# Hybrid layer with a 32-expert MoE on one core: the expert rows turned by VectorE in squares of 32 in place of TensorE transposes

## The chip, the core and the metric

One core of a Trainium2 chip runs the whole layer in one launch. The metric is the device time of that launch in microseconds. The engines that matter here are TensorE (PE, with its weight loads shown apart as PEld), VectorE (DVE), ScalarE (ACT) and the SyncE queue (SP), which issues nearly all of the DMAs.

## The reference, cut to what matters

The layer is a gated hybrid block (gMLP and windowed attention) for 256 positions of width 1024, followed by a mixture of experts: each of the 256 rows goes to its 4 best of 32 experts. All weights are f32. What the change touches is the expert part:

```python
xb = h_pad[slot_tok].reshape(n_blocks, MOE_BLOCK, d)      # rows gathered by expert
def expert_block(args):
    xblk, e = args
    gu = xblk @ w_gate_up[e] + b_gate_up[e]               # 1024 -> 2048
    g = jnp.minimum(gu[:, :D_FF], SWIGLU_LIMIT)
    u = jnp.clip(gu[:, D_FF:], -SWIGLU_LIMIT, SWIGLU_LIMIT)
    hid = g * jax.nn.sigmoid(SWIGLU_ALPHA * g) * (u + 1.0)
    return hid @ w_down[e] + b_down[e]                    # 1024 -> 1024
```

The results are added back to the rows with their gate weights, and a final RMSNorm follows.

## The kernel before

**Stages.** The first 320 us compute the conditioning, the gated block, the router and its tables. Then come the experts, about 1293 us into the span, and a short tail (RMSNorm, store).

**Blocks.** The kernel gathers rows in blocks of 32 (`BM`). With these inputs there are 50 blocks for 32 experts, taken expert by expert; an expert has one to five blocks. Since a block has only 32 rows, each product is cut into four column quarters (`NG` = 4) which run side by side on TensorE in tiles of 128x32: quarter q of the output columns lies in PSUM partitions 32q to 32q+31. So one block's gate-up result is 128 partitions x 512 (256 gate columns, 256 up columns) and its hidden rows `hid` are 128x256. Quarter q holds columns 256q to 256q+255.

**One block on PE** (function `expert`): 8 gate-up steps over the 128-row chunks of the contraction (line 1700), each of 4 matmuls of 512 columns (in f32 each is two MATMUL instructions, 64 in all); the bias (1707); `combine` of the previous block into the accumulator (1663); `gather` of the next block's rows by a one-hot matrix (1645); two transposes of the combine map `selg` (1720); two transposes of `hid` (1725); `gather_T`, two transposes of the gathered rows `xe` (1651); 8 down steps (1735, 64 instructions).

**The other engines in a block.** DVE turns the gate-up result into `hid` (1270 to 1277), copies the gathered rows to `xe` (1280), copies the combine map (1284) and scales the down result (1286). ACT computes the sigmoid (748), then copies the transposed `hid` from PSUM to `hidT` (751) and the transposed rows to `xT` (755). `hidT` and `xT` are the stationary operands of the down and gate-up products.

**Weights.** Each expert has 12 pieces of 1 MB (8 of gate-up, 4 of down), all 384 loaded by SP in order into 22 slots (`SLOTS`) of SBUF. Lines 373 and 379 issue a gate-up or a down piece. A slot is refilled when its piece has been used in the *last* block of its expert: SP waits on `gu_used` or `down_used` for that count (`refill`, `used`). Until an expert's last block, its 12 slots are held.

**The start of the experts.** DVE builds the tables: the block map (1177 and around), the slots of each row (1185 to 1187, twice), the expert of each block (1194, 1196, event `table_ready`), and the order of the experts (`last_is_least`, 1203 to 1241, event `order_ready`), on which SP's refills wait. DVE works its instructions in the order written. At the same time PE gathers block 0 (1645), ACT copies it (740), PE turns it (1651) and ACT copies it to `xT` (742).

Of the kernel before, what the change touches and what calls it, by code (L numbers as in the profile page):

```python
# [15 lines left out]
P = 128  # L16
D = 1024
# [20 lines left out]
HW = D // NG  # L38
KG = HW // P
QR = 32  # L40
# [11 lines left out]
          "down_used", "ex_ready", "exp_done", "g_ready", "gates_ready", "gt_done", "gT_ready",  # L52
          "gu_used", "h2_ready", "heads_ready", "hid_ready", "hidT_ready", "hot_ready", "ht_done", "hT_parts",
          "mask_ready", "merged_ready", "mod_col_ready", "modT_done", "mT_parts", "negm_ready", "negtop_ready",
# [3 lines left out]
          "u_ready", "v_gelu", "var_ready", "vec_steps", "vn_ready", "vp_ready", "w_lower_dve", "w_lower_pool",  # L58
          "w_upper_ready", "ws_masked", "x2_ready", "xe_ready", "xg_done", "xn_ready", "xt_done", "xT_ready",
          "y_out", "y_ready", "yaT_parts", "ybT_parts")  # L60


def bass_hybrid_layer(nc, x, c, positions, w_ada, b_ada, g_norm1, w_in, b_in, ln_v_g, ln_v_b,
# [46 lines left out]
    with ctx:  # L110
# [68 lines left out]
        rope_room = spare[:, 1024:1536]  # L179
        xT = mod[:, 8:10, :].rearrange("p i (q n) -> p i q n", q=NG)  # L180
        y_sb = mod[:, 0:2, :].rearrange("p a b -> p (a b)")
        hidT = mod[:, 6:8, :].rearrange("p i (q n) -> p i q n", q=NG)
        gt2 = mod[:, 10:12, :].rearrange("p a b -> p (a b)")
# [27 lines left out]
        onehot = cut(BM // 2).bitcast(BF16)  # L211
        xe = cut(HW)
        gT = cut(TILES * P)
# [351 lines left out]
        def _(act):  # L565
# [167 lines left out]
            for t in range(TILES):  # L733
# [4 lines left out]

            act.wait_ge(ev("xg_done"), 1)
            act.activation(xe, banks[6][:, 0:HW], ACT.Copy).then_inc(ev("xe_ready"), 1)  # L740
            act.wait_ge(ev("xt_done"), 1)
            act.activation(xT.rearrange("p i q n -> p (i q n)"), banks[6][:, 0:KG * P], ACT.Copy)\
               .then_inc(ev("xT_ready"), 1)
            act.wait_ge(ev("table_ready"), 1)
            total = act.value_load(table[0:1, TOTAL_AT:TOTAL_AT + 1], min_val=1, max_val=GMAX - 1)
            with act.Fori(0, total) as g:
                act.wait_ge(ev("g_ready"), g + 1)
                act.activation(g_sig, g_cap, ACT.Sigmoid, scale=ALPHA).then_inc(ev("sig_ready"), 1)  # L748

                act.wait_ge(ev("ht_done"), g + 1)  # L750
                act.activation(hidT.rearrange("p i q n -> p (i q n)"), banks[7][:, 0:KG * P], ACT.Copy)\
                   .then_inc(ev("hidT_ready"), 1)

                act.wait_ge(ev("xt_done"), g + 2)
                act.activation(xT.rearrange("p i q n -> p (i q n)"), banks[6][:, 0:KG * P], ACT.Copy)\
                   .then_inc(ev("xT_ready"), 1)

# [9 lines left out]
        def _(dve):  # L767
# [381 lines left out]
            def gather_map(g, slots):  # L1149
# [99 lines left out]
            with dve.Fori(0, total) as g:  # L1249
# [50 lines left out]
        def _(pe):  # L1300
# [340 lines left out]
            def gather():  # L1641

                for t in range(TILES):
                    for q in range(NG):
                        last = pe.matmul(banks[6][q * BM:(q + 1) * BM, 0:HW], sel[:, t, :], h2[:, t, q * HW:(q + 1) * HW],  # L1645
                                         start=(t == 0), stop=(t == 1), skip_group_check=True)
# [25 lines left out]
            z_put(last, "etab")  # L1672
            pe.wait_ge(ev("xe_ready"), 1)
            gather_T()
            pe.wait_ge(ev("bias_part_ready"), 4)
# [4 lines left out]
            def expert(e, s, turns):  # L1680


                def piece(i):
                    at = PIECES * s + i
                    pe.wait_ge(slot_in[at % SLOTS], turns * 16 + (16 * (at // SLOTS) + 16))
                    return store(at % SLOTS).rearrange("p (a n) -> p a n", a=2)

# [4 lines left out]
                with pe.Fori(0, blocks) as b:  # L1692
# [4 lines left out]
                    for k in range(KC):  # L1697
                        w = piece(k)
                        for q in range(NG):
                            last = pe.matmul(banks[4][q * BM:(q + 1) * BM, :], xT[:, k % KG, k // KG, :],  # L1700
                                             w[:, :, q * HW:(q + 1) * HW],
                                             start=(k == 0), stop=(k == KC - 1), skip_group_check=True)
                        last.then_inc(ev("gu_used"), 1)
                        if k == 0:
                            for a in range(2):
                                for q in range(NG):
                                    pe.matmul(banks[4][q * BM:(q + 1) * BM, a * HW:(a + 1) * HW], onehot,
                                              bias_parts[a][:, q * HW:(q + 1) * HW], start=False, stop=False,
                                              skip_group_check=True)
# [12 lines left out]

                    pe.wait_ge(ev("hid_ready"), g + 1)
# [4 lines left out]
                    gather_T()  # L1728

                    pe.wait_ge(ev("hidT_ready"), g + 1)  # L1730
                    for i in range(KC // 2):
                        w = piece(KC + i)
                        for k in (2 * i, 2 * i + 1):
                            for q in range(NG):
                                last = pe.matmul(banks[7][q * BM:(q + 1) * BM, 0:HW], hidT[:, k % KG, k // KG, :],  # L1735
                                                 in_groups(w[:, k % 2, :])[:, q],
                                                 start=(k == 0), stop=(k == KC - 1), skip_group_check=True)
# [38 lines left out]
```

## Time and profile before

| | us |
|---|---|
| median of 3 runs (lowest to highest) | 1309.48 (1308.46 to 1310.32) |
| the profiled execution's own time | 1308.77 |
| its span, first to last instruction | 1307.0 |
| PE busy | 1067.9 (82%) |
| DVE busy | 440.1 (34%) |
| ACT busy | 202.4 (15%) |
| bytes read from HBM | 470.98 MB, 361 GB/s over the span |

What lies outside of the span is 1.8 us. The 40 slices of the profile's page are 32.7 us each. The shares of busy time are averages over stages with different limits: PE is busy four fifths of the time, but in the expert stage the DMA engines are at 416 to 418 GB/s in most slices. Releasers of waits are inferred, and matmul ends are modelled.

### The profile page before, as it was taken

How to read it: one execution, taken by the hardware profiler on the slowest of the kernel's cores; microseconds unless marked ns; L12 is line 12 of the kernel's file. 1: busy time of each engine (PE TensorE's matmuls, PEld its weight loads, DVE VectorE, ACT ScalarE, POOL GpSimd, SP SyncE). 2: the span in 40 equal slices, each digit the busy share in tenths (PEclk: the TensorE clock that was granted, in tenths of full speed). 3: DMA queues.
4: the chain of work that ended last, by engine and by line, in shares of the span. 5: the costliest groups of instructions: out<-in, count | busy, mean ns of one | idle time of the engine just before them, and what ended most of it. 6: DMA issues, size and time to landing. Idle time of an engine off the chain costs nothing.

```text
span 1307.0 us, 26543 instructions
## 1 busy us (share of the span) xinstructions
PE 1067.9 (82%) x10210; PEld 495.3 (38%) x10211; DVE 440.1 (34%) x1057; ACT 202.4 (15%) x376; POOL 93.2 (7%) x41
## 2 busy tenths in 40 slices
PE   3689999996999768675799999899776679966784
PEld 1457677883343213111244434343211124421231
DVE  1588588876332112111132322223211113211122
ACT  2112033133111101000021112021100001200011
POOL 0154344300000000000000000000000000000000
PEclk9799999996999769877999999999878879987887
DMA  8897865778999999999979999929999997999996
GB/s 305 254 336 260 312 229 213 218 291 324 384 415 416 416 418 417 417 418 416 416 292 417 417 416 418 417 99 399 416 417 417 418 417 301 417 418 416 417 417 262
DMA packets 113523, 473.22 MB, mean 362 GB/s; under 512 B 12832, under 2 KB 16800, under 8 KB 80544
## 3 DMA queue, kind: packets, MB, share of 16 engines
q1 hardware_dynamic: 110880, 469.03, 89.9%
q10 hardware_dynamic: 2560, 3.02, 0.9%
q8 instruction: 60, 0.98, 0.3%
q14 instruction: 23, 0.19, 0.0%
HBM read 470.98 MB, written 1.05 MB: 361 GB/s over the span
## 4 chain that ended last, share of the span: by engine, by line
PE 34%; SPq 30%; DMA 27%; issue 4%; DVE 3%; ACT 2%; POOL 1%; ACTq 0%; DVEq 0%
SPq L379 13%; SPq L373 12%; PE acc L1338 11%; DMA gate_up<-in_w_down_dram 10%; PE bank L1700 10%; DMA gate_up<-in_w_gate_up_dram 6%; PE bank L1735 5%; DMA down<-in_w_gate_up_dram 3%; DMA down<-in_w_down_dram 2%; DMA gate_up<-in_w_ada_dram 2%; DMA x_sb<-in_w_gate_up_dram 1%; PE acc L1663 1%; DMA room<-in_w_gate_up_dram 1%; PE bank L1645 1%; SPq L368 1%
## 5 line engine op out<-in xcount | busy, mean ns | idle before, releaser
L1700 PE MATMUL bank<-gate_up,mod 128*32 128x512 f32 x2512 | 345.7, 673 | 103.0 <-DMA gate_up<-in_w_gate_up_dram 84.3
L1700 PEld LDWEIGHTS bank<-gate_up,mod 128*32 128x32 f32 x2512 | 75.9, 115 | 313.5 <-DMA gate_up<-in_w_gate_up_dram 178.3
L1735 PE MATMUL bank<-gate_up,mod 128*32 128x256 f32 x2528 | 152.5, 385 | 29.4 <-DMA gate_up<-in_w_down_dram 25.9
L1338 PE MATMUL acc<-gate_up_r 128*128 128x512 f32 (+1 forms) x544 | 136.9, 397 | 15.7 <-DVE gate_up_r L777 12.2
L748 ACT ACTIVATE front<-front 128x256 f32<-128x256 f32 x50 | 20.8, 417 | 743.6 <-DVE front L1270 743.6
L1270 DVE TENSOR_SCALAR front<-bank 128x256 f32<-128x256 f32 x50 | 21.2, 425 | 325.1 <-PE bank L1700 325.1
L1338 PEld LDWEIGHTS acc<-gate_up_r 128*128 128x128 f32 x544 | 100.1, 192 | 44.1 <-issue 21.6
L1735 PEld LDWEIGHTS bank<-gate_up,mod 128*32 128x32 f32 x2528 | 75.5, 110 | 94.9 <-DMA gate_up<-in_w_down_dram 39.0
L1286 DVE TENSOR_TENSOR mod<-bank,mod 128x256 f32<-128x256 f32 x50 | 21.2, 425 | 244.4 <-PE bank L1735 244.4
L348 POOL TENSOR_TENSOR gate_up_r<-gate_up,gate_up_r 128x2048 fp32r<-128x2048 f32 (+1 forms) x14 | 88.7, 6339 | 116.6 <-DVE gate_up_r L777 116.6
L1700 PE MATMUL bank<-down,mod 128*32 128x512 f32 x448 | 62.6, 671 | 18.6 <-DMA down<-in_w_gate_up_dram 16.1
L1190 DVE TENSOR_SCALAR front<-front 128x2 f32 x100 | 22.9, 229 | 154.0 <-issue 152.5
L1338 PE MATMUL acc<-gate_up_r,down_r 128*128 128x512 f32 (+1 forms) x272 | 66.7, 388 | 0.0
L1663 PE MATMUL acc<-mod,front 32*128 32x256 f32 x816 | 65.3, 439 | 0.5 <-DVE mod L1286 0.5
L748 ACT ACT_TABLE_LOAD x50 | 64.2, 1283 | 1.7 <-issue 0.8
L1663 PEld LDWEIGHTS acc<-mod,front 32*128 32x128 f32 x816 | 40.8, 205 | 52.7 <-issue 49.5
L1645 PE MATMUL bank<-h,front 128*32 128x256 f32 x816 | 56.0, 393 | 0.5 <-DVE front L1151 0.5
L1338 PEld LDWEIGHTS acc<-gate_up_r,down_r 128*128 128x128 f32 x272 | 51.2, 192 | 10.7
L777 DVE CAST gate_up_r<-gate_up 128x4096 fp32r<-128x4096 f32 (+1 forms) x17 | 42.3, 2488 | 16.0 <-DMA gate_up<-in_w_in_dram 15.2
L348 DVE TENSOR_TENSOR gate_up_r<-gate_up,gate_up_r 128x2048 fp32r<-128x2048 f32 (+2 forms) x17 | 44.3, 2606 | 0.6
L1735 PE MATMUL bank<-down,mod 128*32 128x256 f32 x512 | 31.5, 382 | 11.5 <-DMA down<-in_w_down_dram 11.1
L1700 PEld LDWEIGHTS bank<-down,mod 128*32 128x32 f32 x448 | 13.2, 114 | 57.1 <-DMA down<-in_w_gate_up_dram 33.0
(303 smaller groups left out, 817.1 us busy)
## 6 DMA issues: line engine op xcount, KB each, us to landing
gate_up<-in_w_gate_up_dram SPq DMA_DIRECT2D x186, 1024.0 KB, 20.5
gate_up<-in_w_down_dram SPq DMA_DIRECT2D x96, 1024.0 KB, 23.8
down<-in_w_gate_up_dram SPq DMA_DIRECT2D x46, 1024.0 KB, 20.6
gate_up<-in_w_ada_dram SPq DMA_DIRECT2D x12, 2048.0 KB, 9.0
down<-in_w_down_dram SPq DMA_DIRECT2D x22, 1024.0 KB, 25.6
gate_up<-in_w_in_dram SPq DMA_DIRECT2D x10, 2048.0 KB, 14.2
x_sb<-in_w_gate_up_dram SPq DMA_DIRECT2D x12, 1024.0 KB, 21.7
room<-in_w_gate_up_dram SPq DMA_DIRECT2D x12, 1024.0 KB, 22.1
```

The source lines that it names most:

```text
L348: return eng.tensor_tensor(w_lower[i % RING][:, chunks, 0:cols], ring[i % RING][:, chunks, 0:cols], w_upper[i % 2][:, chunks, 0:cols], ALU ...
L373: eng.dma_start(store(at % SLOTS), w_gu_view[:, bass.ds(e, 1), k, :].rearrange("p a n -> p (a n)"))\
L379: eng.dma_start(store(at % SLOTS).rearrange("p (a n) -> p a n", a=2), w_dn_view[:, bass.ds(e, 1), 2 * i:2 * i + 2, :].rearrange("p a k n - ...
L748: act.activation(g_sig, g_cap, ACT.Sigmoid, scale=ALPHA).then_inc(ev("sig_ready"), 1)
L777: return dve.tensor_copy(dst, src)
L1190: return dve.tensor_scalar(slots, slots_gates[:, bass.ds(e, 1), 0:2].rearrange("p a t -> p (a t)"), slot_base[:, bass.ds(g, 1)], None, ALU ...
L1270: dve.tensor_scalar(g_cap, banks[4][:, 0:HW], LIMIT, None, ALU.min).then_inc(ev("g_ready"), 1)
L1338: last = pe.matmul(bank[:, 0:cols], lhsT[:, k, rows], w[:, k, 0:cols], start=(n == 0 and k == 0), stop=(n == 2 and k == KC - 1))
L1645: last = pe.matmul(banks[6][q * BM:(q + 1) * BM, 0:HW], sel[:, t, :], h2[:, t, q * HW:(q + 1) * HW], start=(t == 0), stop=(t == 1), skip_g ...
L1663: last = pe.matmul(acc[:, q, t * HW:(t + 1) * HW], gT[rows, t * P:(t + 1) * P], y_sb[rows, :], start=False, stop=True, skip_group_check=True)
L1700: last = pe.matmul(banks[4][q * BM:(q + 1) * BM, :], xT[:, k % KG, k // KG, :], w[:, :, q * HW:(q + 1) * HW], start=(k == 0), stop=(k == K ...
L1735: last = pe.matmul(banks[7][q * BM:(q + 1) * BM, 0:HW], hidT[:, k % KG, k // KG, :], in_groups(w[:, k % 2, :])[:, q], start=(k == 0), stop ...
```

## The change

The four transposes of f32 squares of 128x128 in each block are dropped from TensorE. VectorE turns `hid` into `hidT` and the gathered rows into `xT` with its own transpose, which turns each square of 32x32 in place of its own. For the squares to land where the products need them, the columns of the quarters are dealt out differently: quarter q now holds the columns 128c + 32q + n (c counting the 128-column chunks, n from 0 to 31), so it takes runs of 32 columns, one from each chunk, where it took one run of 256. This is `in_squares`. Gate-up, its bias and the gather read their moving operands that way; the down product keeps its columns. ACT's two copies go, `xe` goes, and so do the events `ht_done`, `xt_done` and `xe_ready`.

```diff
+        def in_squares(rows):
+            return rows.rearrange("p (c q n) -> p q c n", q=NG, n=BM)
...
-                act.wait_ge(ev("ht_done"), g + 1)
-                act.activation(hidT.rearrange("p i q n -> p (i q n)"), banks[7][:, 0:KG * P], ACT.Copy)\
-                   .then_inc(ev("hidT_ready"), 1)
-
-                act.wait_ge(ev("xt_done"), g + 2)
-                act.activation(xT.rearrange("p i q n -> p (i q n)"), banks[6][:, 0:KG * P], ACT.Copy)\
-                   .then_inc(ev("xT_ready"), 1)
...
+            def rows_T():
+                return dve.transpose(xT.rearrange("p c n -> p (c n)"), banks[6][:, 0:HW])
...
             bias_map(0).then_inc(ev("hot_ready"), 1)
+            dve.wait_ge(ev("xg_done"), 1)
+            rows_T().then_inc(ev("xT_ready"), 1)
...
                 dve.tensor_tensor(hid, hid, g_sig, ALU.mult).then_inc(ev("hid_ready"), 1)
+                dve.wait_ge(ev("hid_ready"), g + 1)
+                dve.transpose(hidT.rearrange("p c n -> p (c n)"), hid).then_inc(ev("hidT_ready"), 1)
                 dve.wait_ge(ev("xg_done"), g + 2)
-                dve.tensor_copy(xe, banks[6][:, 0:HW]).then_inc(ev("xe_ready"), 1)
+                rows_T().then_inc(ev("xT_ready"), 1)
...
-            def gather_T():
-                for i in range(KG):
-                    last = pe.transpose(banks[6][:, i * P:(i + 1) * P], xe[:, i * P:(i + 1) * P], ident[:, :])
-                last.then_inc(ev("xt_done"), 1)
...
-                            last = pe.matmul(banks[4][q * BM:(q + 1) * BM, :], xT[:, k % KG, k // KG, :],
-                                             w[:, :, q * HW:(q + 1) * HW],
+                            last = pe.matmul(banks[4][q * BM:(q + 1) * BM, :], xT[:, k, :],
+                                             in_squares(w)[:, q],
...
-                    for i in range(KG):
-                        last = pe.transpose(banks[7][:, i * P:(i + 1) * P], hid[:, i * P:(i + 1) * P], ident[:, :])
-                    last.then_inc(ev("ht_done"), 1)
-                    pe.wait_ge(ev("xe_ready"), g + 2)
-                    gather_T()
                     pe.wait_ge(ev("hidT_ready"), g + 1)
```

PE within one block, from the end of gate-up to the down product, before:

```order
L1700 MATMUL bank<-gate_up,mod 32x512 x28
L1663 MATMUL acc<-mod,front 128x256 x8
L1715 REGISTER_ALU
L1645 MATMUL bank<-h,front 32x256 x8
L1720 MATMUL bank<-ident,front 128x128 x2
L1725 MATMUL bank<-ident,front 128x128 x2
L1651 MATMUL bank<-ident,front 128x128 x2
L1735 MATMUL bank<-gate_up,mod 32x256 x32
```

and the same place in the change (its line numbers are its own):

```order
L1692 MATMUL bank<-gate_up,mod 32x512 x28
L1657 MATMUL acc<-mod,front 128x256 x8
L1707 REGISTER_ALU
L1644 MATMUL bank<-h,front 32x256 x8
L1712 MATMUL bank<-ident,front 128x128 x2
L1720 MATMUL bank<-gate_up,mod 32x256 x32
```

The two pairs of transposes between the one of `selg` and the down product are gone. DVE in one block, from the gate-up result to the down result, before:

```order
L1270 TENSOR_SCALAR front<-bank 128x256
L1271 TENSOR_SCALAR front<-bank 128x256
L1177 ISA
L1177 TENSOR_SCALAR front<-front 96x32
L1274 SCALAR_TENSOR_TENSOR front<-front 128x256
L1277 TENSOR_TENSOR front<-front 128x256
L1279 REGISTER_ALU
L1280 COPY front<-bank 128x256
L1284 COPY front<-bank 128x256
```

and in the change:

```order
L1266 TENSOR_SCALAR front<-bank 128x256
L1267 TENSOR_SCALAR front<-bank 128x256
L1170 ISA
L1170 TENSOR_SCALAR front<-front 96x32
L1270 SCALAR_TENSOR_TENSOR front<-front 128x256
L1273 TENSOR_TENSOR front<-front 128x256
L1276 STREAM_TRANSPOSE mod<-front 128x256
L1278 REGISTER_ALU
L1167 STREAM_TRANSPOSE mod<-bank 128x256
L1283 COPY front<-bank 128x256
```

One transpose has come in behind the making of `hid`, and the copy to `xe` has become a transpose to `xT`. At the start of the experts DVE has in the change:

```order
L1173 SCALAR_TENSOR_TENSOR front<-front 128x64
L1174 MEMSET front 32x16
L1170 TENSOR_SCALAR front<-front 96x32
L1167 STREAM_TRANSPOSE mod<-bank 128x256
```

The last of these four is new; it stands between the block map and the slots of each row, and waits for the gather of block 0.

## Rows read from the trace of the kernel before

**Rows 1.** The page, part 2: GB/s moved in each fortieth of the span.

```profile
GB/s 305 254 336 260 312 229 213 218 291 324 384 415 416 416 418 417 417 418 416 416 292 417 417 416 418 417 99 399 416 417 417 418 417 301 417 418 416 417 417 262
```

**Rows 2.** Windows: length; PE, PEld, DVE, ACT, POOL busy; PEclk, DMA share, GB/s.

```profile
865.00:880.00 15.00, 14.93 (x200) 6.69 (x196) 4.25 (x14) 2.60 (x5) 0.00 (x0) 1.00 0.00 0
```

**Rows 3.** Chain that ended last, at three stretches: start us, us, what.

```profile
644.36 1.07 PE bank L1735 x16
...
655.65 3.66 PE bank L1735 x64
...
669.54 3.66 PE bank L1735 x64
...
674.27 6.01 PE bank L1700 x56
...
836.47 1.07 PE bank L1735 x16
...
849.61 3.66 PE bank L1735 x64
...
863.49 3.66 PE bank L1735 x64
...
877.37 3.66 PE bank L1735 x64
...
882.11 6.01 PE bank L1700 x56
...
1072.96 1.07 PE bank L1735 x16
...
1084.25 3.66 PE bank L1735 x64
...
1098.13 3.66 PE bank L1735 x64
...
1102.87 6.01 PE bank L1700 x56
```

**Rows 4.** Waits of the SP queue: who for whom, us in total, times, longest.

```profile
SPq L379 <- PE bank L1700: 123.9, 11, 47.0
```

**Rows 5.** Timeline of one block: start, us, engine line op, count, idle before.

```profile
812.61 1.07 PE L1645 MATMUL bank<-h,front 128*32 128x256 f32 x16
812.93 0.43 DVE L1277 TENSOR_TENSOR front<-front 128x256 f32<-128x256 f32 x1
...
813.75 0.42 DVE L1280 COPY front<-bank 128x256 f32<-128x256 f32 x1 [0.39 <-PE bank L1645]
...
813.89 0.38 PE L1725 MATMUL bank<-ident,front 128*128 128x128 f32 x2
...
814.23 0.44 PE L1651 MATMUL bank<-ident,front 128*128 128x128 f32 x2
814.30 0.38 ACT L751 ACTIVATE mod<-bank 128x256 f32<-128x256 f32 x1 [1.76 <-PE bank L1725]
...
814.74 0.83 PE L1735 MATMUL bank<-gate_up,mod 128*32 128x256 f32 x9
```

**Rows 6.** Timeline at the start of the experts, all engines.

```profile
321.88 0.18 DVE L1185 SCALAR_TENSOR_TENSOR front<-front 128x32 f32<-128x32 f32 x1
...
322.27 0.38 ACT L740 ACTIVATE front<-bank 128x256 f32<-128x256 f32 x1 [3.77 <-PE bank L1645]
...
325.90 1.93 PE L1700 MATMUL bank<-gate_up,mod 128*32 128x512 f32 x8 [2.45 <-issue]
...
328.81 0.21 DVE L1241 TENSOR_TENSOR table<-front 1x64 int32<-1x64 f32 x1
...
331.43 1.08 SPq L379 DMA_DIRECT2D gate_up<-in_w_down_dram  x2
```

**Rows 7.** Windows at the same place, columns as in rows 2.

```profile
330.00:332.00 2.00, 2.00 (x24) 0.49 (x16) 0.40 (x1) 0.00 (x0) 0.00 (x0) 1.00 0.12 49
```

**Rows 8.** Timeline near the end: four VectorE operations of 512 columns each.

```profile
1301.21 2.73 DVE L1294 SCALAR_TENSOR_TENSOR h<-acc,sm,gate_up 128x512 f32<-128x512 f32 x4
```

More of the change, by code:

```diff
@@ L38 @@
 HW = D // NG
-KG = HW // P
 QR = 32
@@ L52 @@
           "down_used", "ex_ready", "exp_done", "g_ready", "gates_ready", "gt_done", "gT_ready",
-          "gu_used", "h2_ready", "heads_ready", "hid_ready", "hidT_ready", "hot_ready", "ht_done", "hT_parts",
+          "gu_used", "h2_ready", "heads_ready", "hid_ready", "hidT_ready", "hot_ready", "hT_parts",
           "mask_ready", "merged_ready", "mod_col_ready", "modT_done", "mT_parts", "negm_ready", "negtop_ready",
@@ L58 @@
           "u_ready", "v_gelu", "var_ready", "vec_steps", "vn_ready", "vp_ready", "w_lower_dve", "w_lower_pool",
-          "w_upper_ready", "ws_masked", "x2_ready", "xe_ready", "xg_done", "xn_ready", "xt_done", "xT_ready",
+          "w_upper_ready", "ws_masked", "x2_ready", "xg_done", "xn_ready", "xT_ready",
           "y_out", "y_ready", "yaT_parts", "ybT_parts")
@@ L179, in bass_hybrid_layer @@
         rope_room = spare[:, 1024:1536]
-        xT = mod[:, 8:10, :].rearrange("p i (q n) -> p i q n", q=NG)
+        xT = mod[:, 8:10, :].rearrange("p i (c n) -> p (i c) n", n=BM)
         y_sb = mod[:, 0:2, :].rearrange("p a b -> p (a b)")
-        hidT = mod[:, 6:8, :].rearrange("p i (q n) -> p i q n", q=NG)
+        hidT = mod[:, 6:8, :].rearrange("p i (c n) -> p (i c) n", n=BM)
         gt2 = mod[:, 10:12, :].rearrange("p a b -> p (a b)")
@@ L211, in bass_hybrid_layer @@
         onehot = cut(BM // 2).bitcast(BF16)
-        xe = cut(HW)
         gT = cut(TILES * P)
@@ L736, in _ @@
             act.activation(gT, bank[:, 0:TILES * P], ACT.Copy).then_inc(ev("gT_ready"), 1)
-            act.wait_ge(ev("xg_done"), 1)
-            act.activation(xe, banks[6][:, 0:HW], ACT.Copy).then_inc(ev("xe_ready"), 1)
-            act.wait_ge(ev("xt_done"), 1)
-            act.activation(xT.rearrange("p i q n -> p (i q n)"), banks[6][:, 0:KG * P], ACT.Copy)\
-               .then_inc(ev("xT_ready"), 1)
             act.wait_ge(ev("table_ready"), 1)
@@ L1644, in gather @@
                     for q in range(NG):
-                        last = pe.matmul(banks[6][q * BM:(q + 1) * BM, 0:HW], sel[:, t, :], h2[:, t, q * HW:(q + 1) * HW],
+                        last = pe.matmul(banks[6][q * BM:(q + 1) * BM, 0:HW], sel[:, t, :], in_squares(h2[:, t, :])[:, q],
                                          start=(t == 0), stop=(t == 1), skip_group_check=True)
                 last.then_inc(ev("xg_done"), 1)
-            def gather_T():
-                for i in range(KG):
-                    last = pe.transpose(banks[6][:, i * P:(i + 1) * P], xe[:, i * P:(i + 1) * P], ident[:, :])
-                last.then_inc(ev("xt_done"), 1)
             def combine():
@@ L1672, in _ @@
             z_put(last, "etab")
-            pe.wait_ge(ev("xe_ready"), 1)
-            gather_T()
             pe.wait_ge(ev("bias_part_ready"), 4)
@@ L1685, in piece @@
                     pe.wait_ge(slot_in[at % SLOTS], turns * 16 + (16 * (at // SLOTS) + 16))
-                    return store(at % SLOTS).rearrange("p (a n) -> p a n", a=2)
+                    return store(at % SLOTS)
                 if s:
@@ L1707, in expert @@
                                     pe.matmul(banks[4][q * BM:(q + 1) * BM, a * HW:(a + 1) * HW], onehot,
-                                              bias_parts[a][:, q * HW:(q + 1) * HW], start=False, stop=False,
+                                              in_squares(bias_parts[a])[:, q], start=False, stop=False,
                                               skip_group_check=True)
@@ L1734, in expert @@
                             for q in range(NG):
-                                last = pe.matmul(banks[7][q * BM:(q + 1) * BM, 0:HW], hidT[:, k % KG, k // KG, :],
-                                                 in_groups(w[:, k % 2, :])[:, q],
+                                last = pe.matmul(banks[7][q * BM:(q + 1) * BM, 0:HW], hidT[:, k, :],
+                                                 in_groups(w[:, k % 2 * D:(k % 2 + 1) * D])[:, q],
                                                  start=(k == 0), stop=(k == KC - 1), skip_group_check=True)
```

4 lines of the change are left out of this document (removed).

## The prediction

> **What bounds the kernel now.** I read the bytes per slice first [rows 1]. From slice 11 on, where the experts are under way, the core moves 415 to 418 GB/s in nearly every slice and never more. TensorE is busy most of that time, but each expert's 12 MB take about 30 us at that rate, and a block of PE work takes 13.9 us (669.54 less 655.65) [rows 3], so an expert of one or two blocks is waited for by PE, not by the DMA. The DMA is the bound of the stage. Four slices fall out of line: 292, 99, 399 and 301 GB/s. Against 417 they lack 0.30, 0.76, 0.04 and 0.28 of 32.7 us, some 45 us in which no weights move. In the middle of the longest gap the window shows DMA share 0.00 with PE at 14.93 of 15.00 us [rows 2]. SP's waits say why: its refills wait for PE's gate-up steps, up to 47 us at a time [rows 4]. These are the experts with four or five blocks: all 22 slots are full, and none comes free before the expert's last block. Only there does PE's speed count.
>
> **How many blocks count.** The chain of waits [rows 3] shows the three stretches. Each begins with a down piece of 16 instructions that PE had to wait for (644.36, 836.47, 1072.96), so what PE saved earlier is lost in that wait. It ends when the last block's gate-up steps release slots (about 674, 881 and 1102 us). Whole down products between these points: 2, 3 and 2, the seven rows of 3.66 us. Whatever lets the down product start earlier counts 7 times, not 50 times. In the other 43 blocks it turns into a longer wait for weights, or into slots released to a DMA that is busy anyway.
>
> **Part 1, the transposes in a block: -0.76 us each.** In the block shown [rows 5], `hid` is ready at 812.93 + 0.43 = 813.36. The down product starts at 814.74: between them stand PE's turn of `hid` (813.89), which had queued behind other PE work, PE's turn of the rows (814.23), which waited for DVE's copy to end at 814.17, and ACT's copy, which ended at 814.68. In the change two things must end. On DVE, a transpose of 128x256 starts at about 813.40. No row shows this operation. The nearest rows are 128x256 operations from SBUF and from PSUM, 0.43 and 0.42 us [rows 5]; I take 0.43, which gives 813.83, and with the 0.06 us that PE took to follow DVE here (814.17 to 814.23), 813.89. On PE, the `selg` transposes are past at 813.89, where the first turn of `hid` started. Then the tile shape changes to 128x32, which costs about 0.1: the 16 gather instructions take 1.00 to the next shape (812.61 to 813.61), where by the down rows 16 take 4 x 0.216 = 0.86 (64 in 3.66, 16 in 1.07, so 48 in 2.59). That gives 813.98, and PE's side is the later one. So 814.74 - 813.98 = 0.76. The turn of the rows goes behind that of `hid` on DVE and is done near 814.3; `xT` is wanted only after the down product. DVE's copy of the combine map moves from 814.15 to about 814.3, also in time. ACT has only the sigmoid left, on the path as before. Seven times 0.76 is **-5.3 us**.
>
> The value of that transpose, T, is the term to bound. DVE's side is 813.46 + T, so the saving is 1.28 - T, and at most 0.76. From below T can't help beyond that. From above, if 4-byte data goes through twice, T grows by 256 elements: 512 columns take 2.73 / 4 = 0.68 [rows 8], so T = 0.43 + 0.26 = 0.69 and the saving is 0.59. If four times, T = 1.2 and the saving is 0.08.
>
> The Trainium skill, page "VectorE: DVE Perf Modes", section "The three transpose paths", gives 311 ns for 128 columns of bf16 on VectorE and 390 ns on TensorE, a gain of 0.08 us and no figure for f32. By that difference alone seven blocks would give only 0.6 us; the trace shows that what goes is two copies and two hand-overs more than a transpose.
>
> **Part 2, the moving operands in runs of 32: 0.** Gate-up and gather now read 16 and 8 runs of 128 bytes. Rows of before have runs of 256 and 128 columns alone: the gather reads one run of 256 per instruction, the down product two of 128, and 16 instructions take 1.07 us in both [rows 3, 5]. So the number of runs costs nothing between one and two, and I carry that on to 16. It can't be a gain. As a loss it has no bound from these rows, and it is the first rival.
>
> The Trainium skill, page "Advanced Engine Details and Errata", section "Memory Cachelines", says that SBUF reads run at full rate as long as at least two accesses fall into one 16-byte line. Runs of 128 bytes satisfy that, so by the page the cost is 0; no run here shows it yet.
>
> **Part 3, the start: +0.85 us.** The new wait stands in DVE's chain of tables. DVE reached line 1185 at 321.88; now it waits until the gather of block 0 is done, 322.27 (where ACT's copy started) [rows 6], turns the rows for 0.43 and goes on at 322.73, 0.85 later. Queued behind it is the whole chain to `order_ready` (328.81), for which SP waits, and the table on which PE's first block waits (325.90). SP's first refill is at 331.43, and the DMA idles before it: share 0.12 [rows 7]. Nothing hides this; the DMA streams without a break from there to the first stretch, so the whole shift reaches the end. PE's turn and ACT's copy, which go, were beside this chain. With T = 0.69 the term is 1.1. At least it is about 0.4 (a turn in no time), if the wait stands.
>
> **Part 4, nothing.** The tail (last down piece, norm, store) is untouched. The granted clock in the stretches is 1.00 [rows 2] with PE at work nearly without a break, and four short instructions fewer in 13.9 us leave it so.
>
> **Sum.** -5.32 + 0.85 = -4.5 us. Against the profiled execution's 1308.77 that is 1304.3. That execution lies 0.7 below the median of 1309.48, so for a median I give 1305.0. A measurement of this kernel can tell about 0.2% (2.6 us) from no change.
>
> **Rivals.**
>
> *Short runs slow the moving reads (ends slower).* In the three stretches lie 7 whole gate-up products of 16 groups of four instructions, and 2 groups in each last block, 118 groups of 0.43 us (56 instructions, 14 groups, in 6.01) [rows 3]. The gain of 4.5 us is used up at 38 ns a group, 9%, or 2.7 ns for each of 14 further runs. Four streams now read within the same 512 bytes of a partition, where they were 1 KB apart. At 5 ns a run it is +8.3, 1313; at half rate (+50 us) about 1355. For it: no row has runs under 128 columns. Against it: one and two runs cost the same. 0.10.
>
> *The transpose of f32 takes two passes.* Part 1 gives 7 x 0.59 = 4.1, part 3 1.1: 1306.5. 0.13.
>
> *It takes four passes.* -0.6 + 1.6, so +1.0: 1310.5. From T = 1.08 on the change doesn't pay. 0.04.
>
> *The saving doesn't reach the DMA.* If SP's own steps (table loads before each refill) set the resumption and not PE, or if the DMA gap closes later by what it opens later, only part 3 or little more is left: 1308 to 1310. Against it: SP waits for PE in so many words, up to 47 us [rows 4]. 0.13.
>
> *The forecast:* 1305.0, its own range 1303.5 to 1306.3. 0.60.
>
> **Range and chances.** I leave out the short runs at a real price and the four passes, and little below the forecast: 1303.0 to 1310.0. Faster by over 0.2% means under 1306.9: 0.57 of the forecast and 0.08 of the two passes, 0.65. Slower by over 0.2% (over 1312.1): most of the short runs and a little for what I don't see, 0.13. The rest, 0.22, is within.
>
> **What would show it.** In the block of the changed profile: the down product starts about 0.6 us after `hid`'s last multiplication, the block period within an expert is 13.1 in place of 13.9, STREAM_TRANSPOSE takes 0.4 to 0.5 us, and 56 gate-up instructions still take 6.01 us. At the start: `order_ready`'s write and the first refill 0.8 to 0.9 later. In the page: the same slices below 417 GB/s, their gap shorter by 5 us in sum. A longer gate-up product, or a transpose near 1 us, would prove me wrong; so would an unchanged gap.

## The result, and the profile after

| | before | after |
|---|---|---|
| median, this comparison (lowest to highest) | 1309.07 (1308.46 to 1310.32) | 1300.16 (1299.88 to 1302.20) |
| profiled execution | 1308.77 | 1300.29 |
| its span | 1307.0 | 1298.5 |

The ratio is 0.9936, 95% interval 0.9921 to 0.9951, from four runs of each: 8.9 us less, where the forecast had 4.5 and the range ended at 1303.0. A second set of runs of the same kernel gave 1301.69, so part of the 8.9 us is chance; how much is taken up below.

The page of the changed kernel, part 2, GB/s in each fortieth, to be laid beside [rows 1]:

```profile
GB/s 309 244 337 272 301 227 222 207 290 334 361 416 417 416 416 416 417 417 418 416 311 417 416 417 417 416 169 416 417 417 417 417 418 317 415 417 418 417 417 257
```

The same slices fall out of line: 292 has become 311, 99 and 399 have become 169 and 416, 301 has become 317. At 417 GB/s for a slice of 32.7 us that is 1.5, 6.8 and 1.3 us less of gap: the two outer ones about as forecast (2 x 0.76 = 1.5 each), the middle one three times the forecast (3 x 0.76 = 2.3).

One block of the changed kernel, timeline, beside [rows 5]:

```profile
809.50 1.07 PE L1644 MATMUL bank<-h,front 128*32 128x256 f32 x16
809.82 0.43 DVE L1273 TENSOR_TENSOR front<-front 128x256 f32<-128x256 f32 x1
810.28 0.45 DVE L1276 STREAM_TRANSPOSE mod<-front 128x256 f32<-128x256 f32 x1
...
810.51 0.44 PE L1712 MATMUL bank<-ident,front 128*128 128x128 f32 x2
810.65 0.44 DVE L1167 STREAM_TRANSPOSE mod<-bank 128x256 f32<-128x256 f32 x1
...
810.87 1.50 PE L1720 MATMUL bank<-gate_up,mod 128*32 128x256 f32 x24
811.05 0.42 DVE L1283 COPY front<-bank 128x256 f32<-128x256 f32 x1
```

`hid` is ready at 809.82 + 0.43 = 810.25, its turn takes 0.45, and the down product starts at 810.87, 0.62 after `hid`; before it was 814.74 - 813.36 = 1.38. The chain of waits of the changed kernel at the three stretches, beside [rows 3]:

```profile
645.52 1.07 PE bank L1720 x16
...
656.12 3.59 PE bank L1720 x64
...
669.24 3.59 PE bank L1720 x64
...
833.24 1.07 PE bank L1720 x16
...
843.84 3.59 PE bank L1720 x64
...
856.96 3.59 PE bank L1720 x64
...
870.08 3.59 PE bank L1720 x64
...
1065.75 1.07 PE bank L1720 x16
...
1076.35 3.59 PE bank L1720 x64
...
1089.48 3.59 PE bank L1720 x64
```

A block takes 669.24 - 656.12 = 13.12 (13.88 before), the same seven down products count, and the gate-up products between them take as long as before: the chain has 56 of their instructions at 6.01 us in every block. The start of the experts, beside [rows 6]; the first line is the gather of block 0 in before, the others are of the changed kernel:

```profile
320.27 1.94 PE L1645 MATMUL bank<-h,front 128*32 128x256 f32 x16 [0.54 <-DVE front L1151]
...
320.68 1.94 PE L1644 MATMUL bank<-h,front 128*32 128x256 f32 x16 [0.88 <-DVE front L1140]
...
322.67 0.45 DVE L1167 STREAM_TRANSPOSE mod<-bank 128x256 f32<-128x256 f32 x1 [0.31 <-PE bank L1644]
...
329.94 0.21 DVE L1237 TENSOR_TENSOR table<-front 1x64 int32<-1x64 f32 x1
...
332.57 1.08 SPq L381 DMA_DIRECT2D gate_up<-in_w_down_dram  x2
```

`order_ready` is written 1.13 later and the first refill goes out 1.14 later than before (forecast 0.85). Of this 0.41 lies ahead of the wait: the gather of block 0 began at 320.68 in this execution, before at 320.27. The wait and the turn cost the other 0.72 or so.

**Where the time went.** The trace records when each of the 16 DMA engines lands its part of each 1 MB piece. I worked out, for every piece, the landing of the first and the last engine, and then the shift of the first against the kernel before. Between the stretches, where the DMA streams without a break, this shift stays within about 0.2 us; it changes only at the start and in the three stretches:

```
                 start   stretch 1  stretch 2  stretch 3
after - before   +1.2      -1.4       -7.0       -1.2
forecast         +0.85     -1.5       -2.3       -1.5
```

The four add up to 8.4 of the 8.5 us by which the span is shorter. All of the excess over the forecast, 4.7 us, is in the second stretch. Two things fill it. (I call restart the moment at which TensorE goes on after its wait for the last down piece of a long expert, in that expert's first block.) First, the piece that ends the wait at the second restart (piece 215, the last of the twelve of the five-block expert) lands 4.51 us after its first engine's part in before, and 1.63 us after it in the change. The chain shows the restart at 833.24 in place of 836.47, though the first engine is ahead by only 0.36: 2.9 us. Second, TensorE's granted clock. Before, the chain at the restart reads:

```profile
811.92 24.50 DMA down<-in_w_down_dram
...
836.47 1.07 PE bank L1735 x16
837.54 1.69 PE bank L1700 x8
...
839.66 6.81 PE bank L1700 x56
```

and the windows of the kernel before at the same place (columns as in [rows 2]; the seventh number is the granted clock):

```profile
834.00:838.00 4.00, 1.53 (x20) 0.68 (x24) 0.39 (x1) 0.00 (x0) 0.00 (x0) 0.97 1.01 419
838.00:842.00 4.00, 4.00 (x33) 1.60 (x29) 0.90 (x6) 0.00 (x0) 0.00 (x0) 0.61 1.01 420
```

TensorE had stood idle for the piece (1.53 of 4.00 us busy), at 837.7 the granted clock fell from 2.4 to 1.2 GHz for 3.4 us, and 8 gate-up instructions took 1.69 where they take 0.86. From the restart to the first whole down product it was 849.61 - 836.47 = 13.14 us; in the first stretch, at full clock, 655.65 - 644.36 = 11.29 [rows 3]: 1.85 us lost. In the changed kernel the windows are at 1.00:

```profile
834.00:838.00 4.00, 4.00 (x52) 1.50 (x48) 0.55 (x2) 0.00 (x0) 0.00 (x0) 1.00 1.01 416
838.00:842.00 4.00, 4.00 (x44) 1.44 (x40) 1.76 (x8) 0.08 (x1) 0.00 (x0) 1.00 1.00 416
```

3 x 0.76 + 2.88 + 1.85 = 7.0, as found. That is an account of two executions. Whether the two extra terms belong to the change is what the later experiments ask.

### The profile page after: what moved, and what is told of

Its sections match the earlier page's. It is cut to its first block, busy times and chain, and to the rows that moved or that the text cites. A ratio compares the mean times of both kernels' runs of the same rounds, so it can differ in the third digit from the quotient of the medians.

```text
span 1298.5 us, 26038 instructions
## 1 busy us (share of the span) xinstructions
PE 1049.3 (81%) x10008; PEld 474.0 (37%) x10009; DVE 458.5 (35%) x1108; ACT 163.4 (13%) x274; POOL 93.2 (7%) x41
## 4 chain that ended last, share of the span: by engine, by line
PE 39%; DMA 29%; SPq 24%; issue 3%; DVE 3%; ACT 1%; POOL 1%; ACTq 0%; DVEq 0%
PE bank L1692 13%; PE acc L1337 11%; DMA gate_up<-in_w_down_dram 11%; SPq L381 11%; SPq L375 9%; DMA gate_up<-in_w_gate_up_dram 9%; PE bank L1720 6%; DMA down<-in_w_down_dram 4%; DMA room<-in_w_gate_up_dram 2%; PE acc L1657 2%; PE bank L1644 2%; DMA gate_up<-in_w_ada_dram 2%; DMA down<-in_w_gate_up_dram 1%; DMA gate_up<-in_w_in_dram 1%; PE bank L1359 1%
## 5 line engine op out<-in xcount | busy, mean ns | idle before, releaser
L1692 PE MATMUL bank<-gate_up,mod 128*32 128x512 f32 x2512 | 352.4, 683 | 100.3 <-DMA gate_up<-in_w_gate_up_dram 81.5
L1720 PE MATMUL bank<-down,mod 128*32 128x256 f32 x512 | 33.2, 394 | 13.5 <-DMA down<-in_w_down_dram 13.5
```

The costliest lines, as they stand in the source:

```text
L1692: last = pe.matmul(banks[4][q * BM:(q + 1) * BM, :], xT[:, k, :], in_squares(w)[:, q], start=(k == 0), stop=(k == KC - 1), skip_group_chec ...
```

## The experiments

Four theories are named in the expectations. A and B are about one block, L and U about how many blocks count. A: the saving is the step from `hid` to the down product, so both turns must go. B: each turn saves its own part. L: seven blocks count, and the rest of the gain is the late piece and the clock. U: some twelve blocks count, and the gain is paid by the shorter block alone.

### One part of the change alone

Only the rows: `hid` is turned by TensorE and copied by ACT as before.

```diff
-                dve.tensor_copy(xe, banks[6][:, 0:HW]).then_inc(ev("xe_ready"), 1)
+                rows_T().then_inc(ev("xT_ready"), 1)
...
-                    pe.wait_ge(ev("xe_ready"), g + 2)
-                    gather_T()
```

> The gathered rows are turned by VectorE (also block 0's), hid still goes TensorE, PSUM, ScalarE. Theory A (the saving per block is the step from hid to the down product, and both old turns must go for it): the down product still waits for ScalarE's copy of hidT, so the block period inside an expert stays 13.88 us, and only the start costs +1.1: about 1310.0. Theory B (each turn taken from TensorE saves its own part): period 13.5 and about 1306.5.

Measured: 1308.35 median of 10 runs, ratio 0.9991 (0.9978 to 1.0004), between A's 1310.0 and B's 1306.5. The chain of this kernel in the first stretch:

```profile
656.42 0.39 ACT mod L750
...
656.86 3.66 PE bank L1728 x64
...
670.74 3.66 PE bank L1728 x64
```

The block is 13.88, as before: ACT's copy of `hid` still ends the wait for the down product, so the rows' turn alone saves nothing.

Only `hid`: the rows go by DVE's copy, TensorE and ACT as before; gate-up and its bias read in runs of 32.

```diff
-                    for i in range(KG):
-                        last = pe.transpose(banks[7][:, i * P:(i + 1) * P], hid[:, i * P:(i + 1) * P], ident[:, :])
-                    last.then_inc(ev("ht_done"), 1)
...
+                dve.transpose(hidT.rearrange("p c n -> p (c n)"), hid).then_inc(ev("hidT_ready"), 1)
```

> hid is turned by VectorE, the gathered rows still go VectorE copy, TensorE, ScalarE. Theory A: TensorE's turn of the rows now waits behind VectorE's turn of hid and its copy (about 814.3 in the block shown) and the down product starts at about 814.7 as before: period 13.85, no cost at the start, about 1308.5. Theory B: period 13.4 and about 1305.0.

Measured: 1307.11 (10 runs), ratio 0.9980 (0.9967 to 0.9993). The chain in the first stretch:

```profile
654.67 0.42 DVE front L1283
...
655.13 0.44 PE bank L1654 x2
655.57 3.59 PE bank L1734 x64
...
669.31 3.59 PE bank L1734 x64
```

13.74, a saving of 0.14. DVE copies the rows only after it has turned `hid` (654.30 + 0.45), so TensorE's turn of the rows now waits for DVE and stands in the path in place of `hid`. In the block A holds: 0.00 and 0.14 alone, 0.76 together. Both times lie 1.4 to 1.7 us under those that A gave; the account of all profiles below has where the rows' one gains in its profile, at a restart and not in a block. The 56 gate-up instructions are 6.01 in both kernels.

### The start

The change, with block 0's rows copied by ACT and turned by TensorE, so that DVE doesn't wait.

```diff
-            dve.wait_ge(ev("xg_done"), 1)
-            rows_T().then_inc(ev("xT_ready"), 1)
...
+            pe.wait_ge(ev("xe_ready"), 1)
+            gather_T()
```

> The change, but block 0's rows are copied by ScalarE and turned by TensorE as before, so VectorE's table chain at the start has no wait. Theory A: the 1.15 us at the start reach the end: about 1299.0, with the period at 13.12. Rival: the start is absorbed by a later wait for weights, and the time stays at 1300.2.

> The kernel with the old start once more, unchanged: in its first profile the weights landed 2.1 us earlier than in the change up to the second restart, and 1.2 later after it. Theory L: the first holds again (it is the start's wait), the second doesn't (it was half clock on the restart), so over ten runs it lies at or below the change by about 1 us. Rival: the loss at the restart is there again and the old start brings nothing.

Measured: 1301.85 (4 runs, ratio 0.9940, 0.9919 to 0.9962) and 1302.07 (5 runs, 0.9955, 0.9941 to 0.9969), where the expectations had 1299.0 and about 1 us under the change: both missed. In the profiles the block is 13.12 and the weights run 0.9 ahead of before in the one and 0.8 behind it in the other; in the four other profiles of kernels without the wait (before_again, hid_only and the two padded kernels before, below) they run 0 to 1.3 behind. So the start scatters between executions by as much as the cost in question. The seven profiles with the wait stand 0.9 behind before on average, the seven without it (before itself among them) 0.3, which is in favour of a cost of 0.6 but lies within that scatter. The mean of these nine runs is 1302.0 (within about 1.0 either way, 95%) and that of the 17 runs that have the wait (the change twice, and twice with padding, below) 1301.95 (within about 0.8). The wait's 0.7 us is plain in the trace of after; the times show no sign of it, but they couldn't tell 0.7 from nothing.

### Adding to the block

The change, with two (or four) chained copies of `hid` ahead of its turn on DVE, which do nothing but delay the turn.

```diff
+                dve.tensor_copy(xe, hid).then_inc(ev("dose"), 1)
+                dve.wait_ge(ev("dose"), g * 2 + 1)
+                dve.tensor_copy(xe, hid).then_inc(ev("dose"), 1)
+                dve.wait_ge(ev("dose"), g * 2 + 2)
```

> The change with two added VectorE copies of hid (0.47 us each, one after the other) in front of hid's turn, in each block: the down product starts about 0.8 later, so the period is again 13.9, while the rest of the change stands. Theory L (7 blocks of 0.76 count; the other 4.4 us of the gain come from where a late weight piece and a stretch of half clock happened to fall in the kernel before): 1306 to 1310, by whether a piece lands late at the second restart. Theory U (more than 7 blocks carry the saving to the end, about 12): the period alone decides, and the time is before's plus the start's 1.15, 1310.2, with no late piece.

> As dose2 with four added copies: the down product starts 0.94 later than in dose2, the period is 14.6. Theory L (7 blocks count): 1308.0 + 6.6 = 1314.6. Theory U (12 blocks count): 1308.0 + 11.3 = 1319.3.

Measured: two copies 1308.01 (ratio 0.9993, 0.9984 to 1.0003), block 13.70, within L's range and under U's 1310.2; four copies 1309.96 (1.0007, 0.9994 to 1.0020), block 14.35, under both (L 1314.6, U 1319.3), ten runs each. With four copies the chain of a block is DVE's:

```profile
653.80 0.44 DVE front L1274
...
654.26 0.31 DVE front L1277
...
655.25 0.30 DVE front L1283
655.58 0.46 DVE mod L1285
...
656.08 3.66 PE bank L1729 x64
```

From two to four copies a block grows by 0.65 and the time by 2.0, where seven blocks make 4.5. From the change to two copies a block grows by 0.58 and the time by about 6, where seven blocks make 4.1. Neither theory gives both. The two profiled executions are the fastest of its ten (1306.12) and the slowest of its ten (1312.39); what their traces have is in the account below. The medians are left unexplained: they don't follow the block's length in a straight line.

### The same two kernels again

No edit; the change and the kernel before, with nothing different.

> The change itself once more, unchanged, for a second profile and more times. Theory L: its block period is 13.12 again, and what remains of the gain over the counted 4.2 us differs from profile to profile, since it comes from how late the last of 16 DMA engines delivers at the second restart and whether half clock falls on it: single times spread over 1299 to 1303, the median near 1300.5. Theory U: every profile shows the same 8.5 us, and the times stay within 1 us of each other.

> The kernel before once more, unchanged, for a second profile. Theory L: period 13.88; the 3.3 us lost at the second restart (a piece landing 1.5 late, 1.84 of half clock) need not be there again in that form. Theory U: the second restart looks the same.

Measured: 1301.69 (5 runs, ratio 0.9951, 0.9938 to 0.9965) and 1308.19 (10 runs, 0.9996). The profile of the kernel before repeats itself: spread of piece 215 at 4.30, clock at 1.2 GHz from 837.9 for 3.4 us, a second stretch within 0.2. The profile of the change doesn't. Its first and third stretch gain 1.45 and 1.7 again, but the second 4.7 in place of 7.0, and the windows say why:

```profile
830.00:834.00 4.00, 3.42 (x32) 1.19 (x28) 0.26 (x1) 0.00 (x0) 0.00 (x0) 0.50 1.04 423
834.00:838.00 4.00, 4.00 (x40) 1.32 (x36) 0.84 (x5) 0.00 (x0) 0.00 (x0) 0.76 1.01 418
```

The spread is 1.83, near the 1.63 of the first profile, so the piece came early; but the clock fell at 829.1 for 6.8 us, over the restart. In its chain the first 16 down instructions take 1.94 where they took 1.07. So the full clock at the restart isn't part of the change. The span is the same to 0.2 us all the same (1298.7), since the start of this execution is 1.7 earlier: that both profiles show the same total is luck. The times lie from 1300.40 to 1303.96, not within 1 us of each other as U had it; L had 1299 to 1303 and a median near 1300.5.

### Moving the loads of instructions

In the profile's queues stand 60 loads of instructions of 16 KB in before:

```profile
q8 instruction: 60, 0.98, 0.3%
```

By the trace's records the median of them takes 1.08 us (0.88 to 1.47). The spread of the pieces grows in steps of 0.7 to 1.8 us, nearly all of them within 5 us behind such a load (694.3 behind 691.7, 836.4 behind 833.3; the step at 682.8, right behind a stretch, has none), and falls to 0.1 to 0.5 in each stretch in which the DMA stands still. Most loads make no such step: between 700 and 830 us seven loads come in before, and the spread stays at 3.0. But what the 16 parts of a piece lag behind its first, added up, grows by 1 to 2 us behind each of them (from 13.5 to 15.0 us behind the one at 810.8). That is what would be seen if a load delays one engine at a time and the piece comes later only when it is the one that is last already; the records don't name the engine. In before a load at 833.3 is followed by a step from 3.04 to 4.51 at piece 215 itself. In the change, one at 834.3 comes after the piece has landed. The rest of the difference at piece 215 is older: the spread ahead of it was 3.0 in before and 1.6 in the change since 695 us.

The Trainium skill, page "Runtime: NRT & Kernel Launch", section "Instruction fetch mechanics", says that instructions are refilled in blocks of 16 KiB over a DMA queue and that crossing a block's border is mostly hidden. The size agrees with the trace (60 loads, 0.98 MB); what the traces here add is a delay of weight pieces.

To move the loads, tiny products near the start of TensorE's program, where it waits for its first rows anyway (32 of them, or 96), are added to the kernel before and to the change.

```diff
             pe.wait_ge(ev("consts"), 3)
+            for _ in range(32):
+                pe.matmul(banks[6][0:BM, 0:BM], ident[:, 0:BM], ident[:, 0:BM], start=True, stop=True)
             pe.wait_ge(ev("xn_ready"), TILES)
```

> The kernel before with 32 tiny products of ident by ident (32x32) added to TensorE's program near its start, in time in which TensorE waits for the first rows; nothing else changes, and their result is used by nobody. They only shift where TensorE's later instructions lie, and so when the 16 KB loads of instructions come. In the profiles of the kernel before such a load at 833.3 us falls into the wait for the last down piece ahead of the second stretch (piece 215, whose slowest DMA engine lands 4.51 us behind the fastest), in the change one at 834.3 falls behind it (1.63 us). Theory L (7 blocks times 0.76 us, and the rest of the gain is this piece and the half clock behind it): if the load moves out of 830 to 836 us, the spread of piece 215 is 1.6 to 3.1, the second stretch starts 1.4 to 2.9 us earlier, and the time is 1305.5 to 1308; if it doesn't move, all stays as before, 1308 to 1310. Theory U (the extra gain is paid by the shorter blocks themselves): 1308.5 to 1309.5 either way, the second stretch where it was.

> The same with 96 tiny products (about three times the shift). Theory L: as for 32, a spread of piece 215 of 1.6 to 3.1 and 1305.5 to 1308 where the load of instructions leaves 830 to 836 us, 1308 to 1310 where it does not. Theory U: 1308.5 to 1309.5 either way. Should the 96 products not fit into the wait (some 11 us), all is later by up to 2 us.

> The change with 32 tiny products of ident by ident in the same place. Theory L: part of the second stretch's gain hangs on where the load of instructions falls; with it at 834.3 or later the time stays at 1300 to 1302; with it in 829 to 833 us piece 215 lands with a spread of 3.1 or more and the time is 1301.5 to 1304.5. The gain in the first and third stretch (1.5 us each) and the block of 13.12 us don't move. Theory U: 1300 to 1301.5 wherever the load falls.

> The change with 96 tiny products. As for 32: by L 1300 to 1302 with the load of instructions at 834.3 or later, 1301.5 to 1304.5 with it in 829 to 833 us; by U 1300 to 1301.5 wherever it falls. Up to 2 us more if the 96 products don't fit into the wait.

Measured: before with 32, 1308.09 (ratio 0.9996, 0.9981 to 1.0011); with 96, 1308.38 (0.9995, 0.9983 to 1.0006), ten runs each; the change with 32, 1303.51 (0.9953, 0.9935 to 0.9971); with 96, 1302.42 (0.9946, 0.9928 to 0.9964), four runs each. None of the four medians is in U's ranges (1308.5 to 1309.5 for before, 1300 to 1301.5 for the change); the two of the change are in L's 1301.5 to 1304.5. In the profiles of both padded kernels before no load lies between 828 and 895 us, and the spread of piece 215 is 1.72 and 1.95. The chain of the one with 32:

```profile
811.05 22.98 DMA down<-in_w_down_dram
834.03 0.04 issue
834.08 1.70 PE bank L1737 x16
835.78 1.71 PE bank L1702 x8
...
837.91 6.01 PE bank L1702 x56
```

The restart is 2.4 us earlier than in before, at the same length of block, with the first engine 0.4 later: how late the piece is hangs on where the loads of instructions fall, as L said, and a few instructions 800 us earlier move them. In the change with 32 the load lies at 829.5, ahead of the piece, and the spread steps up to 2.98; with 96 it lies at 832.1, also ahead of it, and the spread stays at 1.95, where L had 3.1 or more. So a load ahead of the piece makes it late only sometimes, as above. But L's 1305.5 to 1308 for the padded kernels before is met by neither median. The profiles, one execution each, show what took the gain there: the clock fell at 1069.9 for 3.4 us, which makes the third stretch 1.3 us longer, and with 96 at 645.3 and, for 6.8 us, at 1071.9 (the stretches 1.5 and 3.0 us longer). With 32 it was low at the very end too. The last down piece and the last `combine`, first in before and then with 32:

```profile
1293.72 1.11 PE bank L1735 x16
...
1295.34 1.19 PE acc L1663 x16
...
1292.82 1.98 PE bank L1737 x16
...
1295.30 2.14 PE acc L1665 x16
```

That is 1.8 us behind the last stretch, and it isn't of the change.

The account of all the profiles, by the same working as above:

```
us against before   start  str. 1  str. 2  str. 3     end  spread 215  clock at 1.2 GHz at a restart
before_again         0.8    0.0    -0.2    -0.1      +0.2    4.30      837.9 (3.4)
before_pad32         0.2   +0.3    -2.9    +1.3      +2.0    1.72      834.4 (3.4), 1069.9 (3.4)
before_pad96         1.3   +1.5    -2.7    +3.0      -0.2    1.95      645.3, 836.4 (3.4), 1071.9 (6.8)
rows_only            1.2    0.0    -2.6    +1.3      -0.1    3.65      1070.7 (3.4)
hid_only             0.0   -0.3    -0.8    -0.2      -0.3    3.21      833.6 (6.8)
dose2                1.6   -0.3    -3.4    -0.5       0.0    1.93      834.6 (3.4)
dose4                0.0   +0.8    -1.3    +1.5      +2.6    1.68      none
after                1.2   -1.4    -7.0    -1.2      -0.1    1.63      none
after_again         -0.5   -1.5    -4.7    -1.7       0.0    1.83      829.1 (6.8)
after_pad32          1.5   -1.5    -3.7    -1.5       0.0    2.98      831.8 (6.8)
after_pad96          1.4   +0.9    -6.7    -1.6       0.0    1.95      643.8 (6.8)
start_old           -0.9   -1.5    -3.5    -1.4      -0.2    3.36      832.8 (3.4)
start_again          0.8   -1.5    -6.8    -1.5      +2.2    1.87      none
```

`end` is what is left of the difference of the spans. Where it is over 2, in before_pad32, dose4 and start_again, the last piece landed later behind its first part than in before (by 0.2 to 1.1 us) and the clock was at 1.2 GHz on the last products, which took 1.3 to 1.8 us longer.

Each cell of a stretch is the sum of three things: the blocks, the spread of the piece and the clock at the restart. For the second stretch I took 3 times the difference of the block, the difference of the spread, and for the clock what the time from the restart to the next down product has over that of an undisturbed restart of the same kernel. That gives each of the cells within 0.2 (in the kernel before with 96, where no restart is undisturbed, with that of before), but for dose4: -1.3 where the sum is -3.3. There TensorE didn't wait for the piece, which had landed at 834.4; the down product that it belongs to began only at 833.86:

```profile
833.86 3.66 PE bank L1729 x64
```

and reached the piece at 836.5. With blocks this long work ahead of the restart is no longer lost in the wait, so the seven are right only as long as TensorE waits there.

Every kernel with the whole change has -1.2 to -1.7 in the first and the third stretch, two blocks of 0.76, with one exception, and there the clock explains it. In the change with 96 the windows at the first restart are:

```profile
640.00:644.00 4.00, 1.91 (x32) 0.71 (x28) 0.00 (x0) 0.00 (x0) 0.00 (x0) 0.98 1.04 420
644.00:648.00 4.00, 3.12 (x32) 1.20 (x28) 0.01 (x1) 0.00 (x0) 0.00 (x0) 0.50 1.02 416
648.00:652.00 4.00, 4.00 (x36) 1.14 (x32) 0.88 (x3) 0.00 (x0) 0.00 (x0) 0.67 1.02 426
```

+0.9 in place of -1.5, so 2.4 us. In the second stretch the change without a fall of the clock is at -6.7 to -7.0, with one at -3.5 to -4.7. Against the padded kernel before with 32, which has the early piece but the low clock, after_again (early piece, low clock) is -1.8 for three blocks of 0.76 = 2.3; the longer fall can account for the 0.5 between. In no profile but dose4's is there need of more than seven blocks, so as an account of the profiles U falls.

## Why the prediction was wrong, step by step

**What bounds the kernel, and how many blocks count:** right. The gaps of the DMA are where they were, and seven blocks count in every profile of before and of the change; with blocks longer by four copies (dose4) they no longer suffice.

**Part 1, -0.76 a block, -5.3 in all:** right. T was 0.445 to 0.447 from SBUF and 0.41 to 0.45 from PSUM, within 0.03 of a copy (0.42), so the rivals of two and four passes fall. The saving is 13.88 - 13.12 = 0.76, and hid_only and rows_only show that it hangs on both turns. That the down product starts 0.62 behind `hid` is the forecast to the hundredth. The down product itself is no shorter: the chain has 3.59 for 3.66 because it counts a piece only from the end of the one ahead; the timeline has the 64 instructions at 3.66 in the changed kernel too (from 810.87).

**Part 2, runs of 32 at no cost:** right; 6.01 us for 56 instructions, two runs of 256 or sixteen of 32. The first rival falls with it. That agrees with what the Trainium skill, page "Advanced Engine Details and Errata", section "Memory Cachelines", says of two accesses to a line.

**Part 3, +0.85:** near in the trace (some 0.7 from the wait and the turn, and 0.4 that this execution was late already). Whether it reaches the end is not shown: the kernels without it take the same time (1302.0 against 1301.95), with an uncertainty over the size of the term.

**Part 4, "The granted clock in the stretches is 1.00":** this is the step that failed. The row behind it was a window in the middle of the second stretch. At the restart of that stretch, some thirty microseconds earlier, the profile of before had the clock at 1.2 GHz (1.69 for 8 instructions, 6.81 for 56). My own [rows 3] had the loss in them, 849.61 - 836.47 = 13.14 against 655.65 - 644.36 = 11.29, and I didn't subtract. It was worth 1.85 us. The term next to it was not in the sum at all: the piece that ended the wait was complete with the last of 16 DMA engines, 4.5 us behind the first, and in the change 1.6 behind, worth 2.9 us. I took the restart as a fixed point that shifts with the first refill, so the sum put at nothing what either could give back. Both moved between kernels, and the clock between executions of one kernel as well. And "the tail is untouched" holds for the change but not for the time: the end of the span differs by up to 1.8 us with the clock.

**The size.** Of the 8.9 us, the profiles give -5.0 for seven blocks, +1.2 for the start, -2.9 for the piece and -1.85 for the clock, -8.55 in all. The 8.9 isn't the change's lasting worth: the 17 runs that have its blocks and its start (the change twice, with 32 and with 96) have a mean of 1301.95, the 30 runs of before_again and the two padded kernels before 1308.44, a difference of 6.5 with about 1.0 either way (95%). The ratios of the three later sets, each against runs of before taken beside it, give 6.1 to 7.1. Of it 4.5 is the sum of parts 1 and 3, or 5.3 if the start is free. The other 1 to 2 us, themselves known to 1 us only, may be fewer or cheaper delays at the restarts: in the four profiles of before and its like the clock is at 1.2 GHz at 7 of 12 restarts, in the six of the whole change at 4 of 18. From so few profiles that is not shown to be of the change. The wait just ahead of a restart tells only part of it. Where it was 2.8 to 3.0 us (second restart of before, before_again and hid_only, the three in which the step of the spread falls on piece 215 itself) the clock was at 1.2 GHz each time; where it was 1.4 to 1.5 us, at 8 of 34 restarts. So the late piece and the clock of before may hang together; no run sets them apart. The medians of the kernels with added copies stay open as well.

## What to carry to other kernels

Where a queue runs dry only at a few places, count the blocks between them; that part of the sum held here wherever TensorE still waited at the restart. But look at each restart for itself, at its clock and at the last of the DMA engines, before you take it as fixed, and widen the range by what they can give back, since an edit elsewhere moves them too. Before a gain of half a per cent is put down to an edit, take the kernel with a few idle instructions added as a second baseline: here two such paddings moved single stretches by up to 3 us and the median by less than 0.4, while the change's own lay 2.3 and 3.4 us above the median of its first four runs.

## What the runs showed of the hardware

- VectorE's transpose of 128x256 f32 in squares of 32 takes 0.445 to 0.447 us from SBUF and 0.41 to 0.45 from PSUM (50 and 51 of them in after), within 0.03 of a copy of that size (0.42).
- Products whose moving operand is read in runs of 32 f32 (128 bytes) run as fast as with runs of 256: 6.01 us for 56 instructions in before, after and hid_only.
- A load of 16 KB of instructions takes 1.08 us (median of 60 in before). Behind it the 16 parts of a 1 MB piece lag, summed, 1 to 2 us more. The lag stays as long as the weights stream without a break, adds up (0.2 to 5.2 us between first and last part of a piece in before), and is gone only after the DMA has stood still.
- Around a restart of TensorE after its wait for the last down piece the clock was at 1.2 GHz for 3.4 or 6.8 us in 14 of 42 cases. From the restart to the next down product that cost 1.3 to 1.9 us for the shorter and 1.8 to 2.9 us for the longer (part of which can lie ahead of the restart), and it came and went between executions of the same kernel.
